# Gate and up products of a feed-forward layer turned round: weight blocks stationary, tokens moving

## The reference

```python
def rms_norm_2(x, gain):
    xf = x.astype(jnp.float32)
    y = xf * lax.rsqrt(jnp.mean(xf * xf, axis=-1, keepdims=True) + EPS)
    return (y * gain.astype(jnp.float32)).astype(x.dtype)

def swiglu(h, w_gate, w_up, w_down):
    return (jax.nn.silu(h @ w_gate) * (h @ w_up)) @ w_down

x = x + swiglu(rms_norm_2(x, ffn_norm[i]), w_gate, w_up, w_down)   # w_gate, w_up: 2048 x 5632, w_down: 5632 x 2048
```

## Time and profile before

| what | value |
|---|---|
| three runs | 1988.24, 1989.16, 1989.25 us (median 1989.16) |
| the profiled execution | 1988.47 us, its span 1986.7 us |
| TensorE busy | 1949.1 us, 98% |
| TensorE weight loads busy | 1601.1 us, 81% |
| VectorE busy | 1246.5 us, 63% |
| ScalarE busy | 1084.6 us, 55% |
| GpSimd busy | 220.6 us, 11% |
| weight transfers in the stage | 512 KB each, 4.2 to 4.4 us from issue to landing |
| first transposes of `fg` to the last | 1308.27 to 1752.57 us |

### The profile page before, as it was taken

The page is one execution under the profiler, slowest core; times in us unless marked ns, Lnnn a source line. Parts: engine busy times, 40 slices in busy tenths (PEclk is TensorE's granted clock), DMA queues, the critical chain, the costliest instruction groups (busy, mean ns, idle before and its releaser), DMA issues.

```text
span 1986.7 us, 26931 instructions
## 1 busy us (share of the span) xinstructions
PE 1949.1 (98%) x9924; PEld 1601.1 (81%) x9924; DVE 1246.5 (63%) x1799; ACT 1084.6 (55%) x1429; POOL 220.6 (11%) x99
## 2 busy tenths in 40 slices
PE   7999989999999999989999999999999999999999
PEld 6888868888787888868888778888888888888887
DVE  5699967554867777786656885545445454444443
ACT  6444456456768586876456785544444444433332
POOL 0899840000000000000000100000000000000000
PEclk9999999999999999999999999999999999999999
DMA  8655546565555454545555445665655655556654
GB/s 285 198 187 185 181 147 190 181 193 169 158 159 155 143 169 148 165 128 176 183 187 160 128 131 166 195 190 188 192 177 186 202 187 191 188 190 194 194 191 159
DMA packets 182844, 352.44 MB, mean 177 GB/s; under 512 B 11616, under 2 KB 12128, under 8 KB 182752
## 3 DMA queue, kind: packets, MB, share of 16 engines
q1 hardware_dynamic: 181184, 350.27, 55.7%
q10 hardware_dynamic: 1568, 0.94, 0.2%
HBM read 349.06 MB, written 2.10 MB: 177 GB/s over the span
## 4 chain that ended last, share of the span: by engine, by line
PE 92%; ACT 3%; DVE 3%; issue 1%; DVEq 0%; DMA 0%; ACTq 0%; SPq 0%
PE acc L412 29%; PE acc L414 28%; PE acc L413 28%; PE T L394 2%; PE T L530 2%; DVE w_lo L1071 1%; ACT w_hi L689 1%; PE T L627 1%; PE T L616 1%; ACT E L885 1%; DVE E L1269 0%; PE T L522 0%; PE T L543 0%; PE T L542 0%; DVEq L1057 0%
## 5 line engine op out<-in xcount | busy, mean ns | idle before, releaser
L1071 DVE TENSOR_TENSOR w_lo<-raw,w_hi 128x1024 fp32r<-128x1024 f32 x568 | 689.5, 1223 | 614.1 <-ACT w_hi L689 607.1
L689 ACT ACTIVATE w_hi<-raw 128x1024 fp32r<-128x1024 f32 x656 | 683.7, 1058 | 523.4 <-PE acc L414 496.6
L412 PE MATMUL acc<-w_hi,h_hi 128*128 128x512 f32 x1888 | 746.2, 395 | 15.6 <-DVE h_lo L1083 12.8
L414 PE MATMUL acc<-w_hi,h_lo 128*128 128x512 f32 x1888 | 736.4, 390 | 0.0
L413 PE MATMUL acc<-w_lo,h_hi 128*128 128x512 f32 x1888 | 736.1, 390 | 0.0
L412 PEld LDWEIGHTS acc<-w_hi,h_hi 128*128 128x128 f32 x1888 | 355.1, 188 | 94.6 <-DVE h_lo L1083 12.8
L414 PEld LDWEIGHTS acc<-w_hi,h_lo 128*128 128x128 f32 x1888 | 355.0, 188 | 75.0
L413 PEld LDWEIGHTS acc<-w_lo,h_hi 128*128 128x128 f32 x1888 | 355.3, 188 | 70.9
L374 POOL TENSOR_TENSOR w_lo<-raw,w_hi 128x1024 fp32r<-128x1024 f32 x80 | 190.0, 2407 | 83.1 <-ACT w_hi L689 82.8
L1126 DVE SCALAR_TENSOR_TENSOR T<-vpad,feat,T 128x256 f32<-128x256 f32 x464 | 182.4, 478 | 0.0
L412 PE MATMUL acc<-w_hi,y_hi 128*128 128x512 f32 x384 | 152.8, 398 | 5.2 <-DVE y_lo L1076 4.8
(11 more groups left out here) (212 smaller groups left out, 1319.3 us busy)
## 6 DMA issues: line engine op xcount, KB each, us to landing
raw<-in_hgrn_w_in_dram SPq DMA_DIRECT2D x160, 512.0 KB, 3.6
raw<-in_conv_w_in_dram SPq DMA_DIRECT2D x96, 512.0 KB, 4.0
raw<-in_ffn_w_gate_dram SPq DMA_DIRECT2D x88, 512.0 KB, 4.4
raw<-in_ffn_w_up_dram SPq DMA_DIRECT2D x88, 512.0 KB, 4.2
raw<-in_ffn_w_down_dram SPq DMA_DIRECT2D x88, 512.0 KB, 4.7
raw<-in_attn_w_qkv_dram SPq DMA_DIRECT2D x40, 512.0 KB, 3.7
raw<-in_conv_w_out_dram SPq DMA_DIRECT2D x32, 512.0 KB, 4.2
raw<-in_hgrn_w_out_dram SPq DMA_DIRECT2D x32, 512.0 KB, 4.8
```

The lines of the kernel that those rows point to most:

```text
L412: nc.tensor.matmul(o, hi[:, kt, a], w_hi[:, slot, kk, :], start=kt == 0, stop=False)
L414: last = nc.tensor.matmul(o, lo[:, kt, a], w_hi[:, slot, kk, :], start=False, stop=kt == p.chunks * CK - 1)
L689: A(w_hi[:, slot, :, :], raw[:, slot, :, :], ACT.Copy).then_inc(hi_ready, 1)
L1071: TT(w_lo[:, slot, :, :], raw[:, slot, :, :], rounded(w_hi[:, slot, :, :]), ALU.subtract).then_inc(split_ready, 1)
```

## The change

In the gate and up stages the operands change sides. A 128x128 block of the weight chunk is stationary and the 256 tokens of `h_hi` or `h_lo` move. The result in `acc` has 128 output channels on the partitions and the tokens along the free axis; each PSUM bank of a pair holds two channel blocks of 256 tokens. The three products are issued as w_hi x hi, w_hi x lo, w_lo x hi.

A per-token scale now runs along the free axis, so 1/rms is needed as a tile that is equal in all partitions: VectorE spreads `rs` over 128 columns (`rd`), TensorE multiplies it with the identity, and ScalarE copies the result to `rsb` (once, in the first group). VectorE multiplies the gate product by `rsb` (`g_scale`, tick 10), ScalarE applies Silu in place (`gate_silu`, tick 13), and VectorE multiplies by the up product and by `rsb` (`u_out`, tick 2 of the next group). `fg` then has the channels on the partitions, as `down` wants them: there is no transpose, and `f_hi` and `f_lo` come straight from it in SBUF, 128x1024 at a time.

```diff
--- before.py
+++ after.py
@@ -247,6 +247,8 @@
 
         f_hi = sb(ctx, "f_hi", [P, FKT, S], F32R)
         f_lo = sb(ctx, "f_lo", [P, FKT, S], F32R)
+        rd = sb(ctx, "rd", [P, TB, P])
+        rsb = sb(ctx, "rsb", [P, S])
 
         acc = ctx.enter_context(nc.psum_tensor("acc", [P, 2, TB, GC], F32))
         T = ctx.enter_context(nc.psum_tensor("T", [P, 4, 512], F32))
@@ -286,7 +288,7 @@
 
             s = sm[:, :, :].rearrange("p a b -> p (a b)")
             return s[:, 4 * P * h + P - 1:4 * P * h + 2 * P], s[:, 4 * P * h + 2 * P:4 * P * h + 4 * P + 1]
-        f_g, f_y, f_T, f_h, f_l = (sem(f"ffn_{s}") for s in ("g", "y", "T", "hi", "lo"))
+        f_rd, f_rT, f_rs, f_s, f_g, f_y, f_h, f_l = (sem(f"ffn_{s}") for s in ("rd", "rT", "rs", "scaled", "g", "y", "hi", "lo"))
         out_ready, out_done = sem("out_ready"), sem("out_done")
 
         def rounded(ap):
@@ -417,6 +419,29 @@
                     for f in (hooks or {}).get(i, ()):
                         f()
 
+            def stream_turned(name, j, hi, lo, hooks=None, need=None):
+
+                p = ph[name]
+                base = p.base(j)
+                for i, (k, c) in enumerate(p.seq):
+                    n, slot, _ = slots(base, i)
+                    if need is not None and k == 0:
+                        need(c)
+                    if c == 0:
+                        pe.wait_ge(pair_free[p.pair(k)], 2 * p.use(j, k))
+                    pe.wait_ge(split_ready, n + 1)
+                    for kk in range(CK):
+                        kt = c * CK + kk
+                        for q in range(GC // P):
+                            o, w = acc[:, p.pair(k), q // 2, (q % 2) * S:(q % 2 + 1) * S], slice(q * P, (q + 1) * P)
+                            nc.tensor.matmul(o, w_hi[:, slot, kk, w], hi[:, kt, :], start=kt == 0 and q % 2 == 0, stop=False)
+                            nc.tensor.matmul(o, w_hi[:, slot, kk, w], lo[:, kt, :], start=False, stop=False)
+                            last = nc.tensor.matmul(o, w_lo[:, slot, kk, w], hi[:, kt, :], start=False,
+                                                    stop=kt == p.chunks * CK - 1 and q % 2 == 1)
+                    last.then_inc(chunk_used, 1)
+                    for f in (hooks or {}).get(i, ()):
+                        f()
+
             def x_turn(s, k, free=None):
 
                 pe.wait_ge(x_done, 4 * (s - 1) + k + 1)
@@ -641,23 +666,21 @@
             stream("att_out", 0, y_hi, hy_lo, early.with_(x_turns("att_out", 3, (a_lo, 8))), lambda c: pe.wait_ge(a_lo, c + 1))
 
 
-            def f_turn(j):
-                pe.wait_ge(f_y, j + 1)
-                if not is_first(j):
-                    pe.wait_ge(f_l, 2 * j)
-                transposes(T01, fg, f_T)
+            def rates_turn():
+                pe.wait_ge(f_rd, 1)
+                for tb in range(TB):
+                    last = nc.tensor.matmul(T[:, 3, tb * P:(tb + 1) * P], rd[:, tb, :], ident[:, :], start=True, stop=True)
+                last.then_inc(f_rT, 1)
 
             def gu(j):
                 if is_first(j):
-                    stream("gate_up", j, h_hi, h_lo, x_turns("att_out", 3, None).later(32), normed(3))
+                    stream_turned("gate_up", j, h_hi, h_lo, x_turns("att_out", 3, None).later(32).put(8, rates_turn), normed(3))
                 else:
-                    stream("gate_up", j, h_hi, h_lo, Hooks().put(3, lambda: f_turn(j - 1)))
+                    stream_turned("gate_up", j, h_hi, h_lo)
             gu(0)
-            gu(1)
-            with pe.Fori(2, FJ) as j:
+            with pe.Fori(1, FJ) as j:
                 gu(j)
-            stream("down", 0, f_hi, f_lo, Hooks().put(3, lambda: f_turn(FJ - 1)),
-                   lambda c: pe.wait_ge(f_l, 2 * (c // 2 + 1)))
+            stream("down", 0, f_hi, f_lo, None, lambda c: pe.wait_ge(f_l, c // 2 + 1))
 
 
         @block.scalar
@@ -1025,20 +1048,21 @@
             stream("att_out", 0, at.later(40).with_(x_norm("att_out", 3)))
 
 
-            def g_out(j):
-                if not is_first(j):
-                    act.wait_ge(f_T, j)
-                evacuate("gate_up", j, 0, 3, fg, ACT.Silu, f_g)
+            def rates_copy():
+                act.wait_ge(f_rT, 1)
+                A(rsb[:, :], T[:, 3, 0:S], ACT.Copy).then_inc(f_rs, 1)
+
+            def gate_silu(j):
+                act.wait_ge(f_s, j + 1)
+                A(flat(fg[:, :, :]), flat(fg[:, :, :]), ACT.Silu).then_inc(f_g, 1)
 
             def f_hi_out(j):
-                act.wait_ge(f_T, j + 1)
-                for b in range(2):
-                    A(f_hi[:, bass.ds(4 * j + 2 * b, 2), :], T[:, b, :].rearrange("p (a b) -> p a b", a=2),
-                      ACT.Copy).then_inc(f_h, 1)
+                act.wait_ge(f_y, j + 1)
+                A(f_hi[:, bass.ds(4 * j, 4), :], fg[:, :, :].rearrange("p a (b c) -> p (a b) c", c=S), ACT.Copy).then_inc(f_h, 1)
 
             def gu(j):
-                at = x_norm("att_out", 3).later(32) if is_first(j) else Hooks().put(5, lambda: f_hi_out(j - 1))
-                stream("gate_up", j, at.put(10, lambda: g_out(j)))
+                at = x_norm("att_out", 3).later(32).put(10, rates_copy) if is_first(j) else Hooks().put(5, lambda: f_hi_out(j - 1))
+                stream("gate_up", j, at.put(13, lambda: gate_silu(j)))
             gu(0)
             gu(1)
             with act.Fori(2, FJ) as j:
@@ -1472,23 +1496,46 @@
             stream("att_out", 0, at.later(40).with_(x_norm("att_out", 3)))
 
 
+            def rates_spread():
+                settle()
+                for tb in range(TB):
+                    last = V.tensor_copy(rd[:, tb, :], rs[:, 3, tb:tb + 1].to_broadcast([P, P]))
+                last.then_inc(f_rd, 1)
+
+            def columns(a):
+                return a.rearrange("p (b c) -> p b c", c=S)
+
+            def rates():
+                return rsb[:, :].unsqueeze(1).to_broadcast([P, 2, S])
+
+            def g_scale(j):
+                if is_first(j):
+                    dve.wait_ge(f_rs, 1)
+                dve.wait_ge(chunk_used, ph["gate_up"].done(j, 0))
+                for b in range(2):
+                    TT(columns(fg[:, b, :]), columns(acc[:, ph["gate_up"].pair(0), b, :]), rates(),
+                       ALU.mult).then_inc(pair_free[ph["gate_up"].pair(0)], 1)
+                settle().then_inc(f_s, 1)
+
             def u_out(j):
                 dve.wait_ge(f_g, j + 1)
                 dve.wait_ge(chunk_used, ph["gate_up"].done(j, 1))
-                for tb in range(TB):
-                    STT(out=fg[:, tb, :], in0=acc[:, ph["gate_up"].pair(1), tb, :], scalar=rs[:, 3, tb:tb + 1], in1=fg[:, tb, :],
-                        op0=ALU.mult, op1=ALU.mult).then_inc(pair_free[ph["gate_up"].pair(1)], 1)
-                settle().then_inc(f_y, 1)
+                for b in range(2):
+                    TT(fg[:, b, :], acc[:, ph["gate_up"].pair(1), b, :], fg[:, b, :],
+                       ALU.mult).then_inc(pair_free[ph["gate_up"].pair(1)], 1)
+                settle()
+                blocks = fg[:, :, :].rearrange("p a (b c) -> p (a b) c", c=S)
+                TT(blocks, blocks, rsb[:, :].unsqueeze(1).to_broadcast([P, 4, S]), ALU.mult).then_inc(f_y, 1)
 
             def f_lo_out(j):
-                for b in range(2):
-                    dve.wait_ge(f_h, 2 * j + b + 1)
-                    kk = bass.ds(4 * j + 2 * b, 2)
-                    low(f_lo[:, kk, :], T[:, b, :].rearrange("p (a b) -> p a b", a=2), f_hi[:, kk, :], f_l)
+                dve.wait_ge(f_h, j + 1)
+                kk = bass.ds(4 * j, 4)
+                low(f_lo[:, kk, :], fg[:, :, :].rearrange("p a (b c) -> p (a b) c", c=S), f_hi[:, kk, :], f_l)
 
             def gu(j):
-                stream("gate_up", j, x_norm("att_out", 3).later(32) if is_first(j) else
-                       Hooks().put(2, lambda: u_out(j - 1)).put(6, lambda: f_lo_out(j - 1)))
+                at = (x_norm("att_out", 3).later(32).put(6, rates_spread) if is_first(j) else
+                      Hooks().put(2, lambda: u_out(j - 1)).put(6, lambda: f_lo_out(j - 1)))
+                stream("gate_up", j, at.put(10, lambda: g_scale(j)))
             gu(0)
             gu(1)
             with dve.Fori(2, FJ) as j:
```

## The result

| kernel | median of its runs, us | against the kernel before |
|---|---|---|
| before | 1989.03 | |
| changed | 2006.92 (2006.68 to 2007.68, 4 runs) | 1.0091, 95% interval 1.0079 to 1.0103 |

The change makes the kernel 18 us slower. 1982 was forecast, and the time lies 25 us above that, inside the range but on the wrong side of no change. It is the time that the first rival gave, 2007.

The account below looks back on a forecast made before the run. TensorE's matmul-to-matmul distance was taken as the bound. Products at 0.1140 us each gave +2.7 us, transposes -10.0, 1/rms +0.45: -6.8 us in sum, so 1982 us, with a range of 1972 to 2010.

Parts of the forecast that it names:

- the first rival: Gate and up products: the excess is fixed per matmul or weight load, not per column; +18.6 us, 2007 us; chance 30%.
- p: Gate and up products: start-to-start distance of 256-column matmuls, taken as 0.1140 us between 0.1117 and 0.1200; break-even 0.1156.
- the second rival: Gate and up products: weight loads no longer hide; some 430 us longer, milder form +61, 2050 us; chance 6%.
- the excess is gone at the 1.2 GHz level: After a wait, 512-column matmuls 0.427 us apart showed no excess; taken as proof that the excess grows with columns.
- The row of L491: An fp32 matmul of 256 columns, records 0.212 us apart with new weights each; read as swaps alone not costing 0.0133.
- the fixed excess: Gate and up products: each matmul pays 0.0133 us whatever its length, so 0.1200 us at 256 columns; chance 30%.
- the Trainium skill's rule: TensorE: a fixed cost per matmul beyond its columns, about 2.5 ns for bf16, the same at 128 and 512 columns.
- two streams that fall into step: After a restart TensorE needs some ten matmuls to settle, which looked like weight load and columns running as two streams.
- Turns: Transposes of the gated product and the slower matmuls behind them, 0.91 us a group over 11 groups: -10.0 us.
- +0.45 for 1/rms: Making 1/rms a tile, once: two fp32 matmuls of 128x128 leaving four records of 0.112, +0.45 us on TensorE.
- The new work and waits on VectorE and ScalarE: Gate and up groups: 2.7 us more VectorE work a group and new waits, covered by idle time; charged at zero.
- The load hidden: Gate and up products: weight loads overlap and can follow at 0.1117 us, so they stay hidden; the lower end for the distance.

Follow-up runs that it names:

- the run without the width: The changed kernel with its products issued as before (tokens stationary, 512 columns moving) and no transposes, result laid out wrongly; 1979.72 us, ratio 0.9953.

## Why the prediction was wrong

The step that failed is the choice of p, the distance between matmuls of 256 columns: the excess of 0.0133 us at 512 columns was taken to shrink with the width, to 0.0073, and it stayed 0.0133. The sum named the break-even, 0.1156 us, and put p at 0.1140; it is 0.1200, its upper bound. With that the sum gives +18.6 us and 2007; 2006.92 was measured. (The working calls the 0.1200 once that of the second rival; it is that of the first.)

- The reason was: the excess is gone at the 1.2 GHz level, so it is no step between matmuls but a feed that falls behind, and grows with the columns. That it is gone there stands (0.427 us for 512 columns). The rest did not follow: at that level one width was read, and one width can't tell a cost that grows with the columns from one that is fixed and shows only at 2.4 GHz. With a block of 32 columns the excess does grow so; with a full block it is 13.3 ns at 256, 320, 384 and 512 columns.
- The row of L491, "weight swaps alone don't cost 0.0133", was read from one fp32 matmul, which takes twice the time for its columns. "No excess" is not quite so (2.4 ns over 22 such matmuls), and as a neighbour for a full-rate stream of 256 columns it misled: swaps at 0.22 us say little on swaps at 0.12, where the full block costs some 3 ns more than the narrow one.
- For the fixed excess stood the Trainium skill's rule and the sight of two streams that fall into step. The rule's form, a fixed cost per matmul from 256 to 512 columns, holds here to about 1 ns with full blocks at 256, 320, 384 and 512 columns, and not at 504 (16.7 ns); its 2.5 ns are 13.3 for fp32r. I gave it 30% and should have given it at least half, because the only size in the trace, 512, fitted both.
- Turns: forecast -10.0, with +0.45 for 1/rms; measured -9.0 together in the run without the width, where -9.55 was said, and 0.91 us a group. Right.
- The new work and waits on VectorE and ScalarE at nothing: right; TensorE waits for neither, and the run without the width shows 43.52 us a group. ScalarE did not pay for the new Silu either.
- The load hidden, with 0.1117 as its own bound: right as far as that bound goes, which is to be seen at 192 and 128 columns; at 256 the load is not what decides, though it may hold a part of the 13.3 ns.

Open is why the excess is what it is: why it is the same at four widths with a full block, why a narrow block makes 512 columns slower, why many distances are whole multiples of 6.67 ns (0.1200, 0.1467, 0.1733, 0.2267) and others are not, and what load and stream share. Reading both operands from other places was not tried, nor fp32r columns against a bf16-sized load.

## What to carry to other kernels

Where TensorE is the bound, count matmuls as well as columns: an fp32r matmul with a full block of 128 and 256 to 512 columns cost its columns at 2.4 GHz plus 13.3 ns here, so halving the width of 512 costs 5.9% of the products, more than eight transposes a group were worth. A turn that trades width for transposes pays only if (added matmuls) x 13.3 ns is less than the transposes, here 192 x 0.0133 = 2.56 us against 0.91. When the sum hangs on one number that no row shows, and its two bounds lie on either side of break-even, the sign is not known, and the measurement to make first is that number. And an excess that was read at one width, at either clock, doesn't say how it changes with the width.

## What was not expected of the hardware

- The excess of fp32r with a full block is the same 13.3 ns at 512, 384, 320 and 256 columns; bf16 has 2.5 ns at 512, 256 and 128, and fp32 2.4 ns a record at 256.
- A stationary block of 32 columns is slower than one of 128 at 512 moving columns, 0.2317 against 0.2267 us, in the same chunk.
- 504 moving columns take as long as 512, with a full block and 0.2267 us.
- The load records of 128 columns last 191 ns with 4-byte weights and 98 with bf16; full fp32r loads followed each other at 0.1117 us.
